# One constant in a semaphore wait on POOL: where the fourth sum of x blocks begins, ahead of a Strassen-like up-projection

## The reference

```python
x = x + jnp.concatenate([attn, pool], axis=-1) @ w_out
up = _dwconv3(_rmsnorm(x, norm2) @ w_up, conv_w, conv_b)      # 1024 -> 5632
gate, val = up[..., :D_FF], up[..., D_FF:]
x = x + (jax.nn.silu(gate) * val) @ w_down                    # 2816 -> 1024
g = jax.nn.sigmoid(_rmsnorm(x, norm3) @ w_ple_gate + b_ple_gate)
x = x + (p @ w_ple_proj) * g
```

## Time and profile before

| what | value |
|---|---|
| median of three runs | 1187.51 us |
| the profiled execution, its own time | 1187.72 us |
| its span, first to last instruction | 1185.9 us |
| PE busy | 97% |
| DVE busy | 66% |
| ACT busy | 45% |
| POOL busy | 26% |
| DMA, mean | 105 GB/s |
| mean granted TensorE clock | 0.997 |

### The profile page before, as it was taken

The page is one execution under the profiler, slowest core; times in us unless marked ns, Lnnn a source line. Parts: engine busy times, 40 slices in busy tenths (PEclk is TensorE's granted clock), DMA queues, the critical chain, the costliest instruction groups (busy, mean ns, idle before and its releaser), DMA issues.

```text
span 1185.9 us, 15948 instructions
## 1 busy us (share of the span) xinstructions
PE 1149.0 (97%) x5252; PEld 921.3 (78%) x5252; DVE 785.1 (66%) x1099; ACT 530.8 (45%) x910; POOL 307.8 (26%) x304
## 2 busy tenths in 40 slices
PE   6999889999999989999999999999999999999996
PEld 4887666665888867888888888888888888888885
DVE  5639877773468898777778777776333563348665
ACT  5412577685223465444544545444332343225342
POOL 0137533232566043332233322320000020002100
PEclk9999999999999999999999999999999999999999
DMA  6520000104663134223131322214444444433341
GB/s 200 197 54 20 12 12 12 37 1 146 210 203 107 54 119 175 90 69 106 53 106 53 106 72 87 94 65 169 149 143 142 151 136 156 134 114 109 105 143 72
DMA packets 121334, 123.99 MB, mean 105 GB/s; under 512 B 7155, under 2 KB 103754, under 8 KB 119498
## 3 DMA queue, kind: packets, MB, share of 16 engines
q1 hardware_dynamic: 120992, 123.33, 32.1%
q10 hardware_dynamic: 298, 0.11, 0.0%
HBM read 98.25 MB, written 25.17 MB: 104 GB/s over the span
## 4 chain that ended last, share of the span: by engine, by line
PE 86%; DVE 9%; ACT 2%; issue 2%; POOL 1%; DMA 0%; DVEq 0%; SPq 0%; POOLq 0%; ACTq 0%
PE ps L264 26%; PE ps L266 26%; PE ps L265 26%; PE ps L708 2%; PE ps L689 2%; PE ps L583 1%; DVE WL L1819 1%; PE ps L700 1%; ACT SF L1110 1%; DVE WDHL L1667 0%; PE ps L561 0%; DVE SF L1918 0%; DVE XL L1524 0%; DVE SF L1926 0%; DVE SF L322 0%
## 5 line engine op out<-in xcount | busy, mean ns | idle before, releaser
L264 PE MATMUL ps<-XH,WH 128*128 128x512 f32 x728 | 290.0, 398 | 5.1 <-DVE WL L299 3.2
L266 PE MATMUL ps<-XH,WL 128*128 128x512 f32 x728 | 284.0, 390 | 0.0
L265 PE MATMUL ps<-XL,WH 128*128 128x512 f32 x728 | 284.0, 390 | 0.0
L294 ACT ACTIVATE WH<-WR 128x1024 fp32r<-128x1024 f32 (+1 forms) x89 | 92.1, 1035 | 299.7 <-PE ps L266 291.5
L299 DVE TENSOR_TENSOR WL<-WR,WH 128x1024 fp32r<-128x1024 f32 (+1 forms) x89 | 114.5, 1286 | 145.6 <-ACT WH L294 145.2
L264 PE MATMUL ps<-GHL,WH 128*128 128x512 f32 x436 | 169.9, 390 | 0.9 <-DVE WL L1819 0.7
L265 PE MATMUL ps<-GHL,WH 128*128 128x512 f32 x436 | 169.6, 389 | 0.0
L266 PE MATMUL ps<-GHL,WL 128*128 128x512 f32 x436 | 169.6, 389 | 0.0
L264 PEld LDWEIGHTS ps<-XH,WH 128*128 128x128 f32 x728 | 137.1, 188 | 36.8 <-issue 3.9
L265 PEld LDWEIGHTS ps<-XL,WH 128*128 128x128 f32 x728 | 137.2, 188 | 29.5 <-issue 2.2
L266 PEld LDWEIGHTS ps<-XH,WL 128*128 128x128 f32 x728 | 137.0, 188 | 28.8
(11 more groups left out here) (222 smaller groups left out, 1963.7 us busy)
## 6 DMA issues: line engine op xcount, KB each, us to landing
WR<-in_w_down SPq DMA_DIRECT2D x44, 512.0 KB, 3.6
TL<-in_w_up SPq DMA_DIRECT2D x48, 256.0 KB, 3.9
g_scratch<-SF SPq DMA_DIRECT2D x22, 512.0 KB, 4.5
SF<-g_scratch SPq DMA_DIRECT2D x44, 256.0 KB, 3.7
WR<-in_w_up SPq DMA_DIRECT2D x40, 256.0 KB, 3.1
WR<-in_w_out SPq DMA_DIRECT2D x16, 512.0 KB, 3.7
XT<-xt_scratch SPq DMA_DIRECT2D x8, 1024.0 KB, 7.0
WR<-in_w_ple_gate SPq DMA_DIRECT2D x16, 512.0 KB, 3.6
```

What stands on the lines that cost most here:

```text
L264: pe.matmul(out, wh, xh, start=first, stop=False, skip_group_check=skip)
L265: pe.matmul(out, wh, xl, start=False, stop=False, skip_group_check=skip)
L266: return pe.matmul(out, wl, xh, start=False, stop=last, skip_group_check=skip)
L294: act.activation(WH[:, ring(n), base:cols, :], WR[:, ring(n), base:cols, :], ACT.Copy).then_inc(w_hi, 1)
```

## The change

POOL's wait ahead of the fourth sum is for `b_lo` at 24 instead of 28: the low halves of piece "6" are done, those of "7" need not be.

```diff
@@ -2288,7 +2288,7 @@
             with pool.Fori(0, KT - 1) as m:
                 squares(1, m, x2_ready, m + (KT + 1), m + (KT + 1))
             root(B_X2 + 1, 4, 5)
-            pool.wait_ge(b_lo, PIECE["7"] + 4)
+            pool.wait_ge(b_lo, PIECE["6"] + 4)
             for k in range(4):
                 pool.tensor_tensor(xt[:, XS[0], 4 + k, :], xt[:, XS[0], 4 + k, :], xt[:, XS[0], k, :], ALU.subtract).then_inc(t4_ready, 1)
             pool.wait_ge(uw_lo, 13)
```

## The result

| | before | changed |
|---|---|---|
| median | 1187.35 us (12 runs) | 1189.8 us (12 runs) |
| lowest and highest | 1186.51 to 1189.69 | 1186.87 to 1190.47 |
| ratio to the kernel before | | 1.0017, 95% interval 1.0009 to 1.0024 |
| profiled execution, its span | 1185.9 us | 1187.8 us |

The changed kernel is slower by some 2 us: the medians are 2.45 us apart, the ratio gives 2.0 us, and its interval leaves out 1 and reaches from 1.1 to 2.8 us.

The account below looks back on a forecast made before the run. DVE's backlog was taken to bound the kernel up to near 451 us, PE after it. 1187.51 plus 2.0 us (+ 2.9 early sums, - 1.42 returned, + 0.5 low clock) gave 1189.5 us, range 1187.7 to 1190.7 us.

Parts of the forecast that it names:

- The bound: DVE's backlog bounds the stretch until near 451 us; behind it PE has no idle time, so a delay stays.
- What the early sums cost DVE: From 413.6 us POOL's sums stretch four two-SBUF-input DVE instructions, 4.28 us less idle 1.32 us: 2.9 us later.
- the idle 1.32 us: DVE's wait for ACT ahead of low half 0 of "7", taken off the 4.28 us of stretching.
- The price of each: Each two-SBUF-input DVE instruction caught by a POOL sum takes 1.75 instead of 0.68 us, 1.07 us more.
- What comes back: The first two low halves of "4" are no longer caught by POOL's sums, so DVE regains 1.42 us.
- The clock under product "7": PE's longer wait ahead of "7" may lower its clock and delay `add_c22` by 0 to 0.8 us; taken 0.5.
- The sum: DVE from low half 3 of "4" on: + 2.9 - 1.42 + 0.5 = + 2.0 us, unchanged to 451 us.
- The gain: Rival: sums cost DVE next to nothing between 413.6 and 420 us, only 1.42 us returns: 1186.1 us, chance 7%.
- "Nothing moves": Rival: DVE's delay is met by a shorter later wait, or another count holds POOL: 1187.5 us, chance 6%.
- The third, slower by more than 0.2%: Rival: at product "7" the full 0.8 us of low clock and up to 1.30 us per caught instruction: 1190.8 us, 24%.

Follow-up runs that it names:

- e6: The kernel before, with POOL waiting for two low halves of "7" instead of four: 1188.73 us, ratio 1.0005.
- e1: The changed kernel with 12 more matmuls ahead of product "7", into a PSUM bank nobody reads: 1189.36 us, ratio 1.0019.
- e2: The changed kernel with POOL's four sums cut to 8 of 512 tokens, the rest left out: 1186.22 us, ratio 0.9991.
- e3: The kernel before with POOL's four sums cut to 8 of 512 tokens, the rest left out: 1186.89 us, ratio 0.9992.
- e7: The kernel before with two blocks of the fourth sum on DVE in its idle time, two left on POOL: 1185.97 us, ratio 0.9988.
- e8: The kernel before with all four blocks of the fourth sum on DVE, none on POOL: 1187.32 us, ratio 0.9995.
- e4: The changed kernel run again unaltered, for a second profile and more runs: 1189.52 us, ratio 1.0019.
- e5: The changed kernel with POOL's four sums replaced by constant fills of the same blocks, the fourth sum left out: 1186.21 us, ratio 0.9982.

## Why the prediction was right, point by point

The forecast was 1189.5 us, 2.0 us more; measured were 1189.8 us: 2.0 us by the ratio, 2.45 by the medians, 2.49 by stage. That the ratio gives just the forecast's 2.0 us is luck; by stage the forecast was 0.5 us short, in two terms of about equal size.

- **The bound.** DVE's backlog up to 451 us, and nothing behind it that swallows a delay: right. The rest is 735.6 us in all eleven rows of the table.
- **What the early sums cost DVE**, forecast 2.9 us: measured 3.14 us (first sum in PSUM at 9.97 instead of 6.83 us behind the first third sum). The size was nearly right, its composition was not. I had four instructions caught, and the idle 1.32 us taken off. In fact the split at 413.45 us was not caught: it went ahead of POOL's first sum, and that lasted 2.29 us instead. Three were caught, 0.96 + 1.09 + 1.08 = 3.13 us over their 0.68, and the idle 1.32 us stayed idle as before, since POOL took its own delay in it. That one caught instruction too many and 1.32 us too much taken off nearly cancel is luck. The price of each, 1.07 us, held here (in e6 two of three cost less). The rule that the prediction takes from the Trainium skill, "SBUF — State Buffer", section "Who interferes with whom", that the one behind is blocked for the whole instruction of the other, would have made it 3.9 us: 3.14 us were measured, and the measurement decides.
- **What comes back**, forecast 1.42 us: from `add_c22` to the steady loop 26.55 us before and 25.12 us changed, 1.43 us.
- **The clock under product "7"**, taken at 0.5 us between 0 and 0.8: 0.78 us in the first profile (3.92 - 3.14), 0.61 us in the second. It was a mis-sized term: my reason, a wait longer than one behind which the clock fell, spoke for the upper bound, and I took the middle. The low clock began 1.0 us behind PE's start of "7" in the first profile and 1.3 us in the second, and held 8 and 7 of the 12 starts of that product to every 0.43 us. e1 shows that it is a separate term and how much of it arrives.
- **The sum**: 3.14 - 1.43 + 0.78 = 2.49 us by stage, against 2.9 - 1.42 + 0.5 = 2.0: 0.24 us of the difference is the early sums, 0.28 us the clock. 2.49 us are 0.21% of 1187.35 us, a little over the 0.2% line, and the two sets of runs come near to it from below (1.0017 and 1.0019).
- **The rivals.** The gain would have needed sums that cost DVE nothing; that state of things exists, in e2, e3 and e7, and is worth 1.2 us and not my 1.4. "Nothing moves" fell with the stage. The third, slower by more than 0.2%, was the full 0.8 us of clock together with dearer instructions: the first half came true and the second did not.

## What to carry to other kernels

A wait that is looser than the data need is not free to tighten: ask what the freed engine will run beside. On POOL, put work that reads SBUF beside DVE instructions that read PSUM, or give DVE a piece of it where DVE idles, as e7 does; an earlier start that meets two-input SBUF instructions of a DVE that is the bound costs up to 1.1 us for each. And for effects under 0.2%, measure from one named row to another in the profile, not from the start of the span.

## What was not expected of the hardware

- Which of the two engines goes first is not fixed by when their instructions start. Behind low half 32, POOL's sum starts 0.21 us behind the first of two splits on DVE and 0.39 us ahead of the second, in all eleven profiles. In the kernel before and in the changed one (both times) POOL goes first: its sum takes 1.60 to 1.62 us and the second split 1.76 to 1.78 us. In the other eight DVE goes first: the split takes 0.68 us and POOL's sum 2.22 to 2.23 us. The three are also those in which the granted clock of TensorE had fallen in this stage, but no run tells whether that has to do with it. At most 0.3 us of the stage hang on it here, since the chain over ACT stands behind it: from `add_c22` to the steady loop the changed kernel takes 25.12 us and, with DVE first, e1 25.38 us.
- The length of one wait of PE did not tell whether the clock falls behind it. At product "4" it fell behind 2.13 us (kernel before) and not behind 1.95 us (e8, granted clock 1.00 from 413 to 452 us); in an earlier stage of e4 it fell at 144.5 us, behind a wait of 1.59 us and within the next one of 0.58 us.
- Three runs out of the 33 of the kernel before beside e1 to e4, and two of 12 of the changed one, took some 2 us less than the others of their kind; e2, e3 and e5 have one such run each (1184.2 us). No profile looked at here is of one of these.
